# A two-block transformer kernel on one core: seven products of quarters in the first block's FFNs

## What is computed

```
h = layer_norm(DEEPNORM_ALPHA * x + heads @ w_o, ln1_g, ln1_b)
ffn = (jax.nn.silu(h @ w_gate) * (h @ w_up)) @ w_down          # 1024 -> 2816 -> 1024, float32
x = layer_norm(DEEPNORM_ALPHA * h + ffn, ln2_g, ln2_b)         # for layers 0 and 1
...
hc = hc + 0.5 * g1c * swiglu(modulate(hc, norm_ffn1, sh1c, sc1c), w_ffn1_in, w_ffn1_out)   # the second block's context
h = h + 0.5 * g3 * swiglu(modulate(h, norm_ffn2, sh3, sc3), w_ffn2_in, w_ffn2_out)         # its last FFN
```

## Time and profile before

| | |
|---|---|
| time, median of 3 runs | 3041.73 us (3041.68 to 3042.47) |
| the profiled execution | 3044.3 us, its span 3042.2 us |
| mean granted clock of TensorE | 0.998 of full speed |
| PE busy | 3005.9 us, 99% of the span, 15546 matmuls |
| DVE, ACT, POOL busy | 1604.1, 1089.2 and 287.2 us |
| f0 on PE | from 283.29 us on |
| f1 on PE | from 935.45 us on |
| f3 on PE | from 2674.03 us on |

### The profile page before, as it was taken

How to read it: one execution, slowest core, us unless ns; L and a number is a source line. 1 busy time by engine, 2 the same in 40 slices (tenths; PEclk the granted TensorE clock), 3 DMA queues, 4 the chain that set the end, 5 groups by cost and what they waited for, 6 DMA issues and landing times.

```text
span 3042.2 us, 36712 instructions
## 1 busy us (share of the span) xinstructions
PE 3005.9 (99%) x15546; PEld 2462.2 (81%) x15546; DVE 1604.1 (53%) x2408; ACT 1089.2 (36%) x1655; POOL 287.2 (9%) x223
## 2 busy tenths in 40 slices
PE   8999999999999999999999999999999999989998
PEld 6767888877667888878888888888888887879997
DVE  4575333354655334362323324576868694466676
ACT  4553222234534233242121124443333335254444
POOL 0233000011233000020000001010101021000000
PEclk9999999999999999999999999999999999999999
DMA  5114432222124422221211212121212123313322
GB/s 186 44 50 159 177 141 106 104 96 77 42 90 181 160 91 87 94 87 52 76 56 65 68 54 99 56 87 59 87 59 87 59 104 125 125 66 102 110 98 83
DMA packets 45059, 285.20 MB, mean 94 GB/s; under 512 B 5135, under 2 KB 5663, under 8 KB 19424
## 3 DMA queue, kind: packets, MB, share of 16 engines
q1 hardware_dynamic: 42480, 269.77, 24.7%
q0 software_dynamic: 2416, 13.09, 1.2%
HBM read 277.04 MB, written 5.79 MB: 93 GB/s over the span
## 4 chain that ended last, share of the span: by engine, by line
PE 92%; DVE 4%; ACT 2%; POOL 1%; issue 1%; DMA 1%; SPq 0%; DVEq 0%; POOLq 0%; ACTq 0%
PE ps L827 26%; PE ps L828 25%; PE ps L829 25%; PE ps L1079 2%; PE ps L1081 2%; PE ps L1080 2%; PE ps L918 2%; PE ps L997 2%; PE ps L1010 1%; PE ps L1024 1%; PE ps L903 1%; DVE CA L2323 1%; DVE wlo L1862 1%; ACT whi L1306 0%; PE ps L909 0%
## 5 line engine op out<-in xcount | busy, mean ns | idle before, releaser
L827 PE MATMUL ps<-A1h,whi 128*128 128x512 f32 x1936 | 767.6, 397 | 9.9 <-DVE A1l L1881 8.1
L829 PE MATMUL ps<-A1h,wlo 128*128 128x512 f32 x1936 | 754.6, 390 | 0.0
L828 PE MATMUL ps<-A1l,whi 128*128 128x512 f32 x1936 | 754.5, 390 | 0.0
L1862 DVE TENSOR_TENSOR wlo<-wraw,whi 128x2048 fp32r<-128x2048 f32 (+2 forms) x221 | 454.9, 2058 | 263.8 <-ACT whi L1306 263.8
L1306 ACT ACTIVATE whi<-wraw 128x2048 fp32r<-128x2048 f32 (+2 forms) x221 | 377.1, 1706 | 477.3 <-PE ps L829 445.4
L827 PEld LDWEIGHTS ps<-A1h,whi 128*128 128x128 f32 x1936 | 364.5, 188 | 92.2 <-issue 14.8
L829 PEld LDWEIGHTS ps<-A1h,wlo 128*128 128x128 f32 x1936 | 363.7, 188 | 76.8
L828 PEld LDWEIGHTS ps<-A1l,whi 128*128 128x128 f32 x1936 | 364.3, 188 | 73.4 <-issue 2.2
L2038 DVE TENSOR_TENSOR SIL<-SIL,ps 128x512 f32<-128x512 f32 (+1 forms) x88 | 54.7, 621 | 452.8 <-PE ps L829 369.8
L1575 ACT ACTIVATE SIL<-ps 128x512 f32<-128x512 f32 (+1 forms) x88 | 47.9, 544 | 547.4 <-PE ps L829 545.6
L2323 DVE SCALAR_TENSOR_TENSOR CA<-YIN,vec,CA 128x512 f32<-128x512 f32 x238 | 191.9, 806 | 6.9
(11 more groups left out here) (431 smaller groups left out, 5357.9 us busy)
## 6 DMA issues: line engine op xcount, KB each, us to landing
wraw<-wstream SPq DMA_DIRECT2D x159, 1024.0 KB, 4.8
MW<-wstream SPq DMA_DIRECT2D x34, 1024.0 KB, 6.4
wraw<-wstream SPq DMA_DIRECT2D x42, 768.0 KB, 4.2
wraw<-wstream SPq DMA_DIRECT2D x34, 640.0 KB, 3.9
wraw<-wstream SPq DMA_DIRECT2D x4, 960.0 KB, 4.7
hk<-gd POOLq DMA_DIRECT2D x1, 2560.0 KB, 15.8
X<-xT SPq DMA_DIRECT2D x4, 512.0 KB, 7.8
sx<-X POOLq DMA_DIRECT2D x1, 2048.0 KB, 7.6
```

Source lines behind the costliest of these rows:

```text
L827: mm(o, l[0], r[0], start=start, stop=False)
L828: mm(o, l[0], r[1], start=False, stop=False)
L829: return mm(o, l[1], r[0], start=False, stop=stop)
L1862: tt(wlo[i_ % 2][:, 0:n], wraw[i_ % 2][:, 0:n], raw(whi[i_ % 2][:, 0:n]), SUB).then_inc(ev("lo", i_).by(dve_wlo), 1)
```

## The change

Four things are done.

1. `SEVEN` names f0 and f1 too: panels 3 to 21 of both are done by seven products. Places for the sums of tokens, for the fifth product (one cell each, f3 has two) and, in f1, a silu ring of one cell instead of two are added.
2. Their norms' `emit` writes the full float32 result into `X` on ACT, and `restore` by POOL behind the first norm of each layer goes.
3. In the panels ahead of the first seven-product panel, f3's included, `mix`, `mixed_high` and `mixed_low` of panel 3 are put ahead of the silu and the gating of panel 2. The high part of one half of the sums then waits for the middle of panel 2 on PE (`upper half read`, signalled after its fourth block of features) and not for its end.
4. The norm of the context goes from ahead of group 2 into the down panels of group 1: squares behind the first of them, the sum on PE behind `f` = 2, and the emission at `f` = 4.

```diff
-SEVEN = {"f3": 3}
+SEVEN = {"f0": 3, "f1": 3, "f3": 3}
...
+        fives = {"f0": tile_ring(R + 117), "f1": tile_ring(96), "f3": tile_ring(R + 80, R + 81)}
+        SIL1 = Ring([Cell(sb("SIL1", [128, 512], T0 + 26)[:, :])], uses, clock)
...
# tensor
+                    if half and k == 3:
+                        last.then_inc(half.by(product), 1)
...
+                        if behind == (g, f):
+                            square_total(("c1",), TA[:, 3, 0:256], SQA, 256)
...
-                    ffn("f1", [("x", opN[l], opHid[l])], lambda: square_total(("c1",), TA[:, 3, 0:256], SQA, 256))
+                    ffn("f1", [("x", opN[l], opHid[l])], behind=(1, 2))
...
# scalar
+                    if whole is X:
+                        ev("x", *key, c).same(ev("whole", op.name, c))
...
-                    e.wait_ge(ev("mixed", name, j, 3 - h), ev("used mix", name, was, h) if was else ev("used", index["gu", name, j] - 1))
+                    e.wait_ge(ev("mixed", name, j, 3 - h), ev("used mix", name, was, h) if was else
+                              ev("upper half read", name) if h else ev("used", index["gu", name, j] - 1))
...
                         if j < SEVEN[name]:
+                            if after:
+                                mixed_high(after, 1)
                             silu(j)
                             for i in (1, 3, 2, 4) if j == 0 else ():
                                 token_high(i)
-                            gated(j, jj, g)
                             if after:
-                                mixed_high(after, 1)
                                 seed(after)
                                 mixed_high(after, 0)
+                            gated(j, jj, g)
+                            if (name, j) in mod_points:
+                                mods(name, j)
                             continue
...
-                emit(opN[l], TA, ("ln1", l), 512, lambda c: v("ln", 32 * l + 8 + c), ("ln1", l, 1))
+                emit(opN[l], TA, ("ln1", l), 512, lambda c: v("ln", 32 * l + 8 + c), ("ln1", l, 1), whole=X)
...
+                def context(g, f):
+                    if (g, f) == (1, 0):
+                        e.do.preload_act_table_set(LN_EXP)
+                        square_context(SQA, TA[:, 3, 0:256], ("c1",), range(8), lambda c: ev("ctx landed"), ev("rs", "ln1", 1))
+                    elif (g, f) == (1, 4):
+                        rstd(OB.of("sq sum", "c1"), TA[:, 3, :], 256, 1024, eps6, ("c1",), OB.of("sq sum", "c1").full)
...
+                        emit(opC, TA, ("c1",), 256, lambda c: mod(0, c, 1))
+                        e.do.preload_act_table_set(SILU)
+
+                seven(f"f{l}", opN[l], opHid[l], SIL1 if l else SILs, context if l else None)
...
# vector
                         if j < SEVEN[name]:
+                            if after:
+                                mix(after)
+                                mixed_low(after, 1)
                             gate(j)
+                            if after:
+                                mixed_low(after, 0)
                             hidden(j, jj, g)
...
+                seven(f"f{l}", opN[l], opHid[l], first_add(l), SIL1 if l else SILs, within=context if l else None)
...
# gpsimd
-                restore(opN[l], ("ln1", l))
```

More of the change, by code:

```diff
@@ L837, in used, with two @@
                 ev("used", p.i).same(full)
-            def two(p, op, tiles, names, ring=PB, k0=0, group=0, early=False):
+            def two(p, op, tiles, names, ring=PB, k0=0, group=0, early=False, half=None):
                 bs = [ring.take(*n) for n in names]
@@ L1095, in mixed_tokens @@
                 def mixed_tokens(i):
-                    return lambda k: tuple(t[:, k, :] for t in tokens_of[name][i])
+                    return lambda k: tuple(t[:, k, :] if len(t.shape) == 3 else t[:, k // 2, k % 2, :] for t in tokens_of[name][i][0:2])
                 def first(j):
@@ L1132, in gates @@
                 if op.n == 512:
-                    two(p, op, (0, 1), [("gate", name, tag, j), ("up", name, tag, j)], early=j == 0)
+                    two(p, op, (0, 1), [("gate", name, tag, j), ("up", name, tag, j)], early=j == 0,
+                        half=ev("upper half read", name) if j == SEVEN.get(name, 0) - 1 else None)
                 else:
@@ L1144, in gates, with ffn @@
                     used(p, b.full)
-            def ffn(name, streams, between=None, beside=None):
+            def ffn(name, streams, beside=None, behind=None):
                 if name in SEVEN:
@@ L1472, in attention, with seven @@
                         b.free.same(ev("vC", l, x[0]))
-            def seven(name, op, hid, ring, last):
+            def seven(name, op, hid, ring, beside=None):
                 def silu(j):
@@ L1493, in token_high @@
                 def token_high(i):
-                    e.wait_ge(ev("tokens", name, i), PB.of("modp", 35).full)
-                    act(tokens_of[name][i][0], tokens_of[name][i][2], ACT.Copy, bias=0.0, scale=1.0).then_inc(
+                    e.wait_ge(ev("tokens", name, i), PB.of("modp", 35).full if name == "f3" else None)
+                    hi, _, whole = tokens_of[name][i]
+                    act(hi, whole if len(hi.shape) == 3 else whole.rearrange("p (a b) c -> p a b c", b=2), ACT.Copy, bias=0.0, scale=1.0).then_inc(
                         ev("tokens hi", name, i).by(act_out), 1)
@@ L1510, in keep_fifth @@
                 def keep_fifth(j):
-                    five, q = OB.of("five", name, j), FIVE.take("five kept", name, j)
+                    five, q = OB.of("five", name, j), fives[name].take("five kept", name, j)
                     e.wait_ge(five.full, q.before)
@@ L1560, in seven @@
                             seed(leader[name, g + 1])
-                        if g == 3:
-                            last(f, "x")
+                        if beside:
+                            beside(g, f)
             def ffn(name, streams, ring, between=None, last=None):
@@ L1633, in scalar @@
                 rstd(OB.of("sq sum", "ln1", l), TA[:, 3, :], 512, 1024, eps5, ("ln1", l), OB.of("total", "ln1", l).full)
-                emit(opN[l], TA, ("ln1", l), 512, lambda c: v("ln", 32 * l + 8 + c), ("ln1", l, 1))
+                emit(opN[l], TA, ("ln1", l), 512, lambda c: v("ln", 32 * l + 8 + c), ("ln1", l, 1), whole=X)
                 e.do.preload_act_table_set(SILU)
[L1637 to L1648, removed]
+                def context(g, f):
[4 more added lines that the diff above has]
+                        rstd(OB.of("sq sum", "c1"), TA[:, 3, :], 256, 1024, eps6, ("c1",), OB.of("sq sum", "c1").full)
+                        e.wait_ge(ev("decay abs"))
+                        act(la, la, ACT.Exp, bias=0.0, scale=-1.0).then_inc(ev("decay exp").by(act_out), 1)
+                        e.wait_ge(*mod_ready(0))
+                        emit(opC, TA, ("c1",), 256, lambda c: mod(0, c, 1))
+                        e.do.preload_act_table_set(SILU)
+                seven(f"f{l}", opN[l], opHid[l], SIL1 if l else SILs, context if l else None)
                 for c in range(8):
@@ L1842, in scalar, with last_squares @@
             e.do.preload_act_table_set(SILU)
-            def last_squares(f, tag):
-                for c in (f, f + 1):
+            def last_squares(g, f):
+                for c in (f, f + 1) if g == 3 else ():
                     square_push(SQD, TD[:, 3, :], ("fin",), c, ev("rs", "ffn2"))
@@ L2048, in ffn, with seven @@
                             adds(name, g, f, tag, streams)
-            def seven(name, op, hid, add, ring, beside):
+            def seven(name, op, hid, add, ring, beside=iter(()), within=None):
                 def mix(j):
@@ L2070, in add_fifth @@
                 def add_fifth(j):
-                    q, two_halves = FIVE.of("five kept", name, j), halves(name, j)[:, 1:4:2, :]
+                    q, two_halves = fives[name].of("five kept", name, j), halves(name, j)[:, 1:4:2, :]
                     e.wait_ge(PB.of("up", name, "x", j).full, q.full)
@@ L2105, in token_low @@
                     e.wait_ge(ev("tokens hi", name, i))
+                    if len(hi.shape) == 4:
+                        lo, whole = (x.rearrange("p (a b) c -> p a b c", b=2) for x in (lo, whole))
                     tt(lo, whole, raw(hi), SUB).then_inc(ev("tokens lo", name, i).by(dve_out), 1)
@@ L2142, in seven @@
                             mixed_low(leader[name, g + 1], 0)
+                        if within:
+                            within(g, f)
                         adds(name, g, f, "x", [("x", op, hid, add)])
```

38 lines of the change are left out of this document (24 added, 14 removed).

## The result

| | median | lowest to highest | ratio to before |
|---|---|---|---|
| before, 4 runs | 3042.10 us | 3041.68 to 3043.29 | |
| after, 4 runs | 3022.37 us | 3021.78 to 3023.58 | 0.9935 [0.9923, 0.9947] |
| forecast | 3005.6 us | range 3002 to 3019 | |

The kernel is faster by 19.7 us, a little over half of the 36.15 of the forecast, and the time lies above the range. The profiled execution took 3023.58 us with a span of 3021.8; its mean granted clock is 0.997.

A forecast was written before the change was run, and what follows sets the result against it. The prediction took PE, busy 99% of the span, to bound the kernel. Its terms, -30.4 - 7.1 + 0.9 + 0.45 = -36.15 us, took 3041.73 to 3005.6 us, with a range of 3002 to 3019.

The forecast's parts named there:

- The panels: In f0 and f1, 38 panels cost 10.08 us each in place of 10.88: 30.4 us less.
- The openings: At the first seven-product panel: f3 loses 1.5 us, not 8.6, so 7.1 less; f0 and f1 together 0.9 more.
- each opening loses as f3's did: Rival, 8%: the new order brings nothing and three openings lose 8.6 us each, 3029.0 us in all.
- The emission's copies: ACT's eight residual copies for each of two norms, ahead of f0 and f1: 0 us, upper bound 2.2.
- two differences: Around the panels of f0 and f1 against f3: `mods` between panels, and one buffer less for the fifth product, costing nothing.
- small waits at the seams: Rival, 15%: 1.4 us at each of ten `mods` points and 2.2 in the emissions, +16 us, 3021.8.
- The context's norm: Emission moved into group 1's down panels: PE waits 0.8 us at panel 12, an earlier 0.35 goes, net 0.45 more.
- Loads: At the ten `mods` points, two `MW` loads and a panel queue: 0 us, upper bound 14.

The follow-up runs named there:

- e4: The kernel after with the old order ahead of panel 3 in all three FFNs (silu and gating of panel 2 first): 3044.82 us, ratio 1.0007.
- e7: The kernel before with the emissions ahead of f0 and f1 writing the full residual on ACT and POOL's restore removed: 3042.62 us, ratio 1.0001.
- e5: e1 with ACT's two row copies ahead of chunks 0 and 1 in place of 0 and 2: 3008.53 us, ratio 0.989.
- e1: The kernel after with f1's pairs of banks starting with banks 2 and 3 in place of 0 and 1: 3010.44 us, ratio 0.9896.
- e2: The kernel after with DVE's `mods` ahead of the emission's fourth chunk, not behind the emission, in both layers: 3015.65 us, ratio 0.9912.
- e3: The kernel before with only the first panels of f0 and f1 put into banks 0 and 1 by name: 3056.14 us, ratio 1.0044.
- e6: e1 with the context's norm back ahead of group 2, its squares behind group 1's last down panel: 3023.48 us, ratio 0.9938.

## Why the prediction was wrong, step by step

*The panels: right.* 10.08 us each was forecast, 10.07 and 10.09 are read. In f1's group 3, from its first panel to its down panels and with the product that is now run ahead, five panels went from 54.4 to 50.4 us: 0.80 each. The Trainium skill, page "TensorE: Matmul & The Clock Gate", section "Back-to-back issue gap", gives a gap for a matmul that stands alone, by which a panel would take 9.17 us, an estimate. The trace after, with 10.08, disagrees as that of before did.

*The openings: right.* In f3 the wait was to fall from 5.21 to 1.0 us and the clock to stay up. PE's timeline and a window over most of the opening, in the kernel after, beside the earlier trace rows:

```profile
2698.07 0.39 PE L1099 MATMUL ps<-T3h,A1h 128*128 128x256 f32 x1 [0.90 <-DVE A1l L2098]
...
2703.10 0.39 PE L1099 MATMUL ps<-T3h,whi 128*128 128x256 f32 x1 [0.46 <-ACT ps L1533]
```

```profile
2695.57:2707.20 11.63, 10.27 (x83) 9.86 (x82) 10.19 (x12) 7.79 (x11) 0.00 (x0) 1.00 0.26 90
```

f3 gained 6.5 of the 7.1: from the first start to the start behind the eighth product it takes 13.39 us, so 1.87 are lost and not 1.5; and the 8.6 of before ran to ACT's release, 0.26 behind that start. In f0 and f1 only the seed's 0.46 is left, as forecast, in a stretch of eight products that takes 12.23 us and not 11.52: 0.7 each where I had 0.46. The rival "each opening loses as f3's did" is what e4 is, and it falls for the change as made.

*The emission's copies: right as priced, and the wrong thing was priced.* For the copies the sum had 0, and e7 shows 0.1 us per FFN at most. The failing step is the sentence ahead of the first term, "The forms are the same as f3's and so is what lies around them, with two differences". There was a third. An FFN in `SEVEN` has its banks pinned by number from panel 0 on, and in f0 and f1 the vectors of `mods` lie in those banks. No term and no rival had it; "small waits at the seams" comes near in time, 3021.8, but places 14 of its 16 us at the ten `mods` points, where PE waits for nothing, and its other 2.2 on ACT ahead of a chunk. What it cost, by stages of e5 against after: f0 1.2 us, the attention's end 2.1, f1 10.1, in all 13.4 of the 13.8 us between the two medians. e1, e2 and e3 show the cause from three sides: other banks, an earlier reader, and the pins alone.

*The context's norm: right in kind.* "PE waits 0.8": 0.82 on the low part that was named, beside the earlier trace rows. DVE's and ACT's rows of the kernel after, then PE's:

```profile
1131.34 1.76 DVE L1893 TENSOR_TENSOR wlo<-wraw,whi 128x1536 fp32r<-128x1536 f32 x1 [1.12 <-ACT whi L1327]
```

```profile
1128.52 1.28 ACT L1677 ACT_TABLE_LOAD   x1
1129.81 1.49 ACT L1327 ACTIVATE whi<-wraw 128x1536 fp32r<-128x1536 f32 x1
```

```profile
1133.15 0.39 PE L1099 MATMUL ps<-A1h,whi 128*128 128x256 f32 x1 [0.82 <-DVE wlo L1893]
```

The high part starts 0.01 us behind the load's end, so a drain of 1.38 us, as the Trainium skill, page "ScalarE: Activation LUTs", section "What ACT_TABLE_LOAD costs", has it, is not seen here either. I had set the move against the placement of before, where it costs 0.45. e6 shows that the placement of before was no longer to be had: beside seven products it costs some 13 us.

*Loads: right.* PE waits for no transfer in f0 to f3, with ten more points at which three loads queue.

*What is left.* e5 is 33.7 us faster than before, where 36.15 was forecast. By stages: f0 13.5 (14.7), f1 13.2 (14.3), f3 6.5 (7.1), the rest 0.5. In f0 three places make up the missing 1.2, within 0.3 us. The opening takes 0.25 more than forecast. Panels 0 and 1 take 0.4 more than before (22.24 and not 21.85). The down panels, without the product that is run inside them, take 0.8 more in all, nearly all of it in the last two groups (27.45 and 27.63, not 27.20 each). In the last group PE catches up with the weights: on ACT a table load of 1.28 us stands ahead of the high parts of the down panels, the low part of the second one ends at 621.87, and its first product starts at 621.92.

## What to carry to other kernels

When a form of work is copied to a second place, price what it takes by name as well as what it computes: for every bank or buffer with a fixed number, list who wrote it last there and which instruction of which engine frees it, and how far down that engine's list this stands. A wait whose releaser is no operand of the waiting instruction (here `small` and `mrow`) is such a claim on a place. And an experiment that sets the new naming alone into the old kernel (e3) tells it from the cost of the work in one run.

## What the runs showed of the hardware

The clock's answer to a gap on PE is no matter of its length alone. Inside the kernels it fell behind every wait of 4.5 to 8.2 us that is shown here, to 0.69 to 0.83 over the stretches shown. It also fell behind the waits of 2.3 us ahead of f1: in the kernel after the second matmul starts 0.54 us behind the first, where 0.31 is the distance in e1, and in e2 matmuls start every 0.43 us from 926.25 to 928.81, where it is 0.23 in e1. Behind the same 1.31 us in f0 it stayed at 1.00 in the kernel after, in e1, e4 and e6, and fell to 0.91 (280 to 300 us) in e2, though PE's list is the same in e2 and the kernel after and only DVE's differs, from the fourth chunk on. The four runs of e2 lie within 1.6 us of each other; why its clock fell is not settled. So the same short wait cost its own length in four kernels and 1.6 us more in another.
